# Value projections of two dilated head groups: weights stationary, then a transpose per token tile

## What is computed

```python
DIL_PAIRS = ((128, 1), (512, 4), (2048, 16))     # three head groups of 4 heads of 64
h = rmsnorm(x, norm_mix)
qa, ka, va, ... = jnp.split(h @ w_in, ...)
for g, (win, dil) in enumerate(DIL_PAIRS):
    rel = dil * np.arange(-half, half + 1)       # keys at the same residue modulo dil
    o, l = dilated_group_attention(qa[:, :, hs], ka[:, :, hs], va[:, :, hs], bias, rel)
oa = sum of the three o, weighted by softmax of the three l
```

## Time and profile before

| | us |
|---|---|
| median of 3 runs | 1426.71 |
| the runs | 1419.69, 1426.71, 1427.45 |
| span of the profiled execution | 1427.5 |
| PE busy in it | 1235.1 |
| DVE, ACT, POOL busy | 627.7, 555.8, 446.3 |

### The profile page before, as it was taken

The page is one execution under the profiler, slowest core; times in us unless marked ns, Lnnn a source line. Parts: engine busy times, 40 slices in busy tenths (PEclk is TensorE's granted clock), DMA queues, the critical chain, the costliest instruction groups (busy, mean ns, idle before and its releaser), DMA issues. The chain is left out here.

```text
span 1427.5 us, 19757 instructions
## 1 busy us (share of the span) xinstructions
PE 1235.1 (87%) x7936; PEld 1139.9 (80%) x7936; DVE 627.7 (44%) x1051; ACT 555.8 (39%) x905; POOL 446.3 (31%) x196
## 2 busy tenths in 40 slices
PE   6989999998899888999999998971889888988870
PEld 3988999797697877999999998961778878887860
DVE  5002111227435354541121132247477777766756
ACT  6223242344454352332122130151465666566632
POOL 2211120131120201221121242233466676666613
PEclk8999999998999999999999999985898999999995
DMA  7520001233111301202212214063598999999937
GB/s 250 163 60 30 30 9 41 85 91 109 46 45 46 89 1 49 62 23 87 67 38 75 66 61 151 31 212 134 165 335 286 329 310 341 317 321 318 341 137 265
DMA packets 158728, 200.39 MB, mean 140 GB/s; under 512 B 11625, under 2 KB 139773, under 8 KB 158654
## 3 DMA queue, kind: packets, MB, share of 16 engines
q1 hardware_dynamic: 151150, 183.41, 39.3%
q0 software_dynamic: 7504, 15.94, 3.2%
HBM read 179.32 MB, written 34.42 MB: 150 GB/s over the span
## 5 line engine op out<-in xcount | busy, mean ns | idle before, releaser
L837 POOL TENSOR_TENSOR w_lo<-raw,w_hi 128x2048 fp32r<-128x2048 f32 (+2 forms) x37 | 152.6, 4124 | 689.5 <-ACT w_hi L975 689.4
L1202 PE MATMUL bank<-hT_hi,w_hi 128*128 128x384 f32 (+1 forms) x592 | 203.6, 344 | 4.0 <-DVE hT_lo L1491 4.0
L1203 PE MATMUL bank<-hT_lo,w_hi 128*128 128x384 f32 (+1 forms) x592 | 200.7, 339 | 0.0
L1204 PE MATMUL bank<-hT_hi,w_lo 128*128 128x384 f32 (+1 forms) x592 | 200.5, 339 | 0.0
L896 POOL TENSOR_TENSOR lo_gate<-raw_gate,hi_gate 128x2048 fp32r<-128x2048 f32 x30 | 139.2, 4641 | 121.0 <-ACT hi_gate L964 120.8
L1202 PE MATMUL bank<-w_hi,hT_hi 128*128 128x256 f32 x528 | 158.5, 300 | 0.0
L1204 PE MATMUL bank<-w_hi,hT_lo 128*128 128x256 f32 x528 | 156.6, 297 | 0.0
L1203 PE MATMUL bank<-w_lo,hT_hi 128*128 128x256 f32 x528 | 156.6, 297 | 0.0
L1748 DVE TENSOR_TENSOR lo_up<-raw_up,hi_up 128x2048 fp32r<-128x2048 f32 x31 | 109.0, 3516 | 53.6 <-ACT hi_up L964 53.5
L1202 PEld LDWEIGHTS bank<-hT_hi,w_hi 128*128 128x128 f32 (+1 forms) x592 | 111.8, 189 | 8.5 <-DVE hT_lo L1491 4.4
L975 ACT ACTIVATE w_hi<-raw 128x2048 fp32r<-128x2048 f32 (+2 forms) x42 | 74.0, 1763 | 103.7 <-PE bank L1204 103.7
(11 more groups left out here) (285 smaller groups left out, 2895.3 us busy)
## 6 DMA issues: line engine op xcount, KB each, us to landing
raw_gate<-in_w_exp_gate SPq DMA_DIRECT2D x32, 1024.0 KB, 7.7
raw_up<-in_w_exp_up SPq DMA_DIRECT2D x32, 1024.0 KB, 10.8
raw_down<-in_w_exp_down SPq DMA_DIRECT2D x32, 1024.0 KB, 6.0
raw<-in_w_in SPq DMA_DIRECT2D x25, 1024.0 KB, 6.0
y_d<-m_y SPq DMA_DIRECT2D x32, 512.0 KB
y_d<-zeros SPq DMA_DIRECT2D x11, 512.0 KB, 7.2
raw<-in_w_in SPq DMA_DIRECT2D x8, 512.0 KB, 5.9
raw<-in_w_proj_b SPq DMA_DIRECT2D x4, 1024.0 KB, 5.0
```

Source lines behind the costliest of these rows:

```text
L837: pool.tensor_tensor(w_lo[:, g % 2, 0:kb, 0:n], raw[:, g % 2, 0:kb, 0:n], w_hi[:, g % 2, 0:kb, 0:n].bitcast(F32), ALU.subtract).then_inc(w ...
L1202: pe.matmul(out, l_hi, r_hi, start=j == 0, stop=False)
L1203: pe.matmul(out, l_hi, r_lo, start=False, stop=False)
L1204: ins = pe.matmul(out, l_lo, r_hi, start=False, stop=j == n - 1)
```

## The change

For a = 1 and 2, v becomes 4 ws steps with contiguous operands. ACT copies their result with by_class into a new buffer vT (two blocks of 128 value columns by 768 tokens in class order, one buffer for both head groups). Then for each token tile a new step vT makes two PE transposes of 128x128 into one bank, and DVE copies the 128x256 result to va. pv of these groups waits for the last vT copy. The first head group's v stays as it was.

```diff
+        elif name == "v" and idx:
+            r = [S(kind="ws", g=n, b=b, s=s, dest=(name, idx)) for b in range(2) for s in range(2)]
+            r += [S(kind="vT", a=idx, i=i) for i in range(NT)]
...
-        elif s.kind in ("hT", "sc", "oaT", "state", "intra", "o", "obT", "router", "rank", "table"):
+        elif s.kind in ("hT", "vT", "sc", "oaT", "state", "intra", "o", "obT", "router", "rank", "table"):
             s.job = jobs.new("dve")
...
+        vT = at("vT", [P, 2, T], F32, 119)
...
-                        if name in ("q", "k"):
+                        if name in ("q", "k", "v"):
-                            x = qk[:, a % 2, s.b + (2 if name == "k" else 0), :]
+                            x = vT[:, s.b, :] if name == "v" else qk[:, a % 2, s.b + (2 if name == "k" else 0), :]
...
-                            first, n = SEQS[0] if s.i < SEQS[1][0] else SEQS[1]
-                            return x[:, first * P:(first + n) * P].rearrange("p (u r) -> p r u", r=n)[:, s.i - first, :]
...
+                elif k == "vT":
+                    evac_done(pe, E_, last_of_group[gnum["v", s.a]])
+                    for c in range(2):
+                        ins = pe.transpose(b_[:, c * P:(c + 1) * P], vT[:, c, s.i * P:(s.i + 1) * P], ident[:, :])
...
-                    evac_done(pe, E_, last_of_group[gnum["v", u.a]])
+                    evac_done(pe, E_, find(kind="vT", a=u.a)[-1].job if u.a else last_of_group[gnum["v", 0]])
...
+                elif k == "vT":
+                    need(dve, E_, mm, s.job + 1)
+                    dve.tensor_copy(va[:, s.a % 2, s.i, :], b_[:, 0:AW]).then_inc(dve_evac, 1)
```

More of the change, by code:

```diff
@@ L1243, in _ @@
                     else:
-                        def tokens(x):
-                            if name != "v" or s.dest[1] == 0:
-                                return x[:, s.i * P:(s.i + 1) * P]
-                            first, n = SEQS[0] if s.i < SEQS[1][0] else SEQS[1]
-                            return x[:, first * P:(first + n) * P].rearrange("p (u r) -> p r u", r=n)[:, s.i - first, :]
+                        tok = slice(s.i * P, (s.i + 1) * P)
                         ins = product3(b_[:, 0:GW],
-                                       [(tokens(x_hi[:, j, :]), tokens(x_lo[:, j, :]), w_hi[:, g % 2, j, :], w_lo[:, g % 2, j, :])
+                                       [(x_hi[:, j, tok], x_lo[:, j, tok], w_hi[:, g % 2, j, :], w_lo[:, g % 2, j, :])
                                         for j in range(kb)], split=mlo_done if name == "out" else None)
+                elif k == "vT":
+                    evac_done(pe, E_, last_of_group[gnum["v", s.a]])
+                    for c in range(2):
+                        ins = pe.transpose(b_[:, c * P:(c + 1) * P], vT[:, c, s.i * P:(s.i + 1) * P], ident[:, :])
                 elif k == "sc":
```

## The result

| | before | after |
|---|---|---|
| median of 4 runs, us | 1427.08 | 1406.32 |
| the runs, us | 1419.69 to 1429.04 | 1400.52 to 1409.97 |
| span of the profiled execution, us | 1427.5 | 1398.7 (its time 1400.52) |
| PE busy in it, us | 1235.1 | 1206.4 |

The changed kernel is faster: the ratio is 0.985, 95% interval 0.9815 to 0.9885, which is 20.8 us by the medians. The two profiled spans lie 28.8 us apart, and some 10 us of that are not the change, as the rows and the table further down show: 7.6 us lie behind the stage that was edited, 3.1 us are the clock at one boundary, and 0.4 us stand ahead on the other side. Of the 28.8 us, 18.5 are left for the change.

The account below looks back on a forecast made before the run. PE was taken to bound the loops over the first and second head group. 20.4 us net PE work, less 1.0 for light stretches and 1.0 for the clock, gave 18.4 us: 1408.3 us, range 1401 to 1416.

Parts of the forecast that it names:

- The bound: Loops over the first and second head group, 96 to 264 us: PE always has work, so PE work removed shortens the end.
- What is removed and added on PE: Value steps in both loops: 57.7 us removed, 34.3 of ws steps and 3.0 of transposes added, net 20.4 us less.
- My upper end of the net, 21: PE work in both loops: the net saving lies between 19.3 and 21 us across the ranges of step times.
- the upper end of the earlier trace: The 24 added PE transposes: 3.4 us from a pt step of two at 0.28 us; 3.0 was taken.
- ACT, DVE, POOL: Copies, evacuations and weight conversion beside PE in the loops: cost nothing, with 4.5 us, one w_lo, as upper bound.
- Light stretches: Ends of both loops, attention with only vT left: PE waits of 1.0 us in total.
- The wait of unit 35: Attention unit near the end of a loop: PE waits 0.5 us between its sc and pt.
- The clock: Ahead of the gate step after the second loop: clock may fall earlier, 1.0 us taken; the 2.28 us wait's cost unchanged.
- More stalls: Light stretches: half a microsecond for each of 12 units, 6.0 us instead of 1.0, giving 1413.3 us; chance 0.15.
- Half clock in the light stretches: Attention and transposes at both loop ends do not hold the clock, PE work doubles: 1428.3 us; chance 0.07.
- No gain at the end: Strided read not what makes the step slow, or a later stage waits for something pinned: 1426.7 us; chance 0.06.
- whole gain and more: Both loops: no stall, no earlier clock fall, 20.4 to 21 us, 1406; chance 0.10, shared with a low median.

Follow-up runs that it names:

- e1_contiguous: The kernel before, with the value projections of the second and third head group reading their stationary tokens contiguously: 1404.11 us, ratio 0.9862.

## Why the prediction was right, by its steps

**The bound.** Right. PE work in the loops came off them one for one: 18.5 and 18.9 us less in the two profiles, clock taken off, with 18.4 predicted. The medians give 20.8 and 21.0, and their intervals (0.9815 to 0.9885 is some 16 to 26 us) hold 18.5 as well; they don't tell the two apart. That 18.4 and 18.5 agree so well is in part luck: the transposes and the light stretches cost 0.9 us more than I took, and the 1.0 us that I charged for the clock was not there.

**What is removed and added on PE.** 57.7 stood, by e1_contiguous and the contiguous steps; 34.3 us was measured. My upper end of the net, 21, was rounded up: 57.7 - 8 x 4.25 - 3.0 is 20.7. The transposes were mis-sized: 3.4 us and not 3.0, since a pair among attention steps costs 0.22 to 0.39 us; the upper end of the earlier trace rows, which I had named and not taken, was the right one. The 275 ns of the Trainium skill (TensorE: Matmul & The Clock Gate, Part 4), taken 24 times, would have made 6.6 us, an estimate; the trace has half. As the length of one transpose the trace agrees with that figure, though here the data are fp32 and there bf16 (shortest, median and longest in ns):

```profile
L1255 PE MATMUL bank<-ident,vT x24: 272/273/329, 165.5 to 244.8; 128*128 128x128 f32 x24
```

But the next matmul starts before that length is over, and what a transpose costs on a busy PE is the distance between starts, 0.11 to 0.20 us here.

**ACT, DVE, POOL.** The work lay beside PE, as said. One thing was missed: at 175.01 a transpose of probabilities waited 0.34 us behind a DVE copy to va. I had allowed 0.3 for such a delay but placed it in the other loop. In the trace the twelve copies took 0.42 us each (shortest, median and longest in ns, then the first and the last start):

```profile
L1515 DVE COPY va<-bank x12: 412/422/426, 165.9 to 245.1; 128x256 f32<-128x256 f32 x12
```

Whether POOL's w_lo would have held them up was not tested: in both stretches with copies POOL did nothing (0.00 us busy in both windows above), and the nearest w_lo began at 247.81. The one row that speaks for it is still that of 267.38 in the earlier trace rows.

**Light stretches.** The wait of unit 35 was forecast at 0.5 us and was 0.50. With the 0.34 and some wider spacing of pv steps all of it is 1.5 us against 1.0. This is worked out: the first score steps of the third group come at 245.55, 18.1 us earlier, and the loops began 0.4 us later, so 18.5 us came off; 57.7 - 34.3 - 3.4 is 20.0, and the two waits leave 19.2. Behind 245.55 no order changed, and with the clock taken off nothing more came off there.

**The clock.** Wrong. I charged 1.0 us for an earlier fall; the light stretches stood at 1.00. I also took the cost of the wait of 2.28 us as unchanged, and it was lower in the kernel after: 4.25 and 5.80 us for the gate step against 6.44, and no loss in the three steps ahead of it against 0.9. It looks like chance rather than the change, for the same wait gave 6.69, 6.57 and 6.30 us, with 0.7 to 0.9 ahead, in kernels that have the new steps too, in whole or for one group, and 5.82 with nothing ahead in e1_contiguous, which has the old ones. Whether its mean differs between before and after, these profiles don't settle.

**The rivals.** More stalls: fell, 0.84 us of waits, 1.5 with the spacing, and not 6. Half clock in the light stretches: fell, with a clock of 1.00 in both windows; the rule of the Trainium skill that the full clock does not engage on transposes (TensorE: Matmul & The Clock Gate, Part 4) is not borne out for 24 of them spread over attention. No gain at the end: fell with the medians, and its cause with e1_contiguous. The "whole gain and more" is the nearest to what the medians show, 20.8 against 20.4 to 21, but not for its reason: the waits were there, and the loops gave 18.5 to 18.9. The 2 us on top of that lie within what the clock and the rest change from one execution to the next.

## What to carry to other kernels

Price a matmul with a gathered operand by the distance between starts and by the length of its weight load, tile by tile; two tiles of one loop that differ only in the step of their read point to the cause before any experiment, and one run with the step alone changed shows it. When such a read is to go, put the reordering into a copy that is made anyway on an engine with time to spare, and not on the other operand of the matmul: there it cost 31 us more. And spread the light steps that replace heavy ones so that latency chains keep their cover, though here that was worth 1 to 3 us in the profiles and nothing that the runs can tell.

## What the runs showed of the hardware

A stationary read of fp32r is as fast with a step of 2 floats as contiguous (3.0 us for 24 matmuls of 256 columns), takes 4.25 us with 3, and 5.6 to 5.7 with 4, 5 and 6. A streamed read takes twice the time with a step of 2, 3 or 4: 0.45 against 0.23 us for 512 columns with a step of 2, 0.46 with 4, and 0.23 against 0.12 for 256 columns with 3. I had expected the streaming side to keep its rate at any step. And a PE wait of 2.28 us always at the same place cost the gate step between nothing (4.25 us) and 2.4 us (6.70), and the three steps ahead of it between nothing and 0.9 us, from execution to execution of like programs.
